# A decoder layer on one core: VectorE reads projection banks ahead of the attention maxima, one weight split moved, unit 1's scores moved into their slab

## The chip, the core and the metric

The kernel runs on one core of a Trainium2 chip. The metric is the device time of one execution in microseconds (us). Before the change it is 679.45 us, the median of three runs (679.43 to 679.52).

## What is computed

One post-norm decoder layer over 512 tokens, model width 1024, float32 in and out. The part of the reference that matters here:

```python
def hybrid_mixer(x, w_in, b_forget, attn_sinks, w_o_fox, w_o_swa, w_out):
    proj = jnp.einsum('bsd,dc->bsc', x, w_in)
    q_f, k_f, v_f, f_logit, q_s, k_s, v_s, g_f, g_s = jnp.split(proj, idx, axis=-1)
    log_f = jax.nn.log_sigmoid((f_logit + b_forget).astype(jnp.float32))
    o_f = forgetting_attention(q_f, k_f, v_f, log_f)        # 8 heads x 64, causal
    qs, ks = apply_rope(q_s, pos), apply_rope(k_s, pos)
    o_s = sliding_window_sink_attention(qs, ks, v_s, attn_sinks)   # 8 q heads, 2 kv heads, window 128
    merged = jax.nn.sigmoid(g_f) * (o_f @ w_o_fox) + jax.nn.sigmoid(g_s) * (o_s @ w_o_swa)
    return jnp.einsum('bsd,de->bse', merged, w_out)

# layer
h = layer_norm(DEEPNORM_ALPHA * h + mix, ln1_g, ln1_b)
ff = (silu(h @ w_gate) * (h @ w_up)) @ w_down
h = layer_norm(DEEPNORM_ALPHA * h + ff, ln2_g, ln2_b)
```

Heads are reshaped from the columns of the projection. The sliding-window softmax takes the maximum of a row and a learned sink, and the sink's exponential joins the denominator.

## The kernel before

Each float32 operand is split in two: a hi part, rounded to the fp32r format that TensorE multiplies (a copy on ScalarE, ACT), and a lo part, the difference (a subtraction on VectorE, DVE). A product is then three matmuls, hi by hi, lo by hi, hi by lo (`mm3`, line 1643).

The weights come as slabs of 128 x 1024 elements. TensorE (PE) works through them in order: slabs 0, 1, 4, 5 give q_s, slabs 2 and 3 k_s, v_s and the forget logits, 6 to 9 q_f, 10 to 13 k_f, 14 to 17 v_f, then gates, output projections and the feed-forward. In slabs 0, 1 and 4 to 13 eight chunks of the model width accumulate in one PSUM bank. ScalarE's `slab_hi` (line 643) and VectorE's `slab_lo` (line 982) prepare slab n+3 in step n; four slabs fit in the ring, and SyncE's queue loads slab n+2 when slab n's lo part is made.

Attention runs beside the projections, in units of one head. There are eight sliding-window units (a = 0 to 7); unit a starts in step 6+a (`unit_step`) and passes through these stages:

- PE in slab 6+a: `scores(a)` (lines 1676, 1681) into banks 2 and 3. For a of 1 and more they wait for the exponentials of unit a-1 (`exp_done`), which read the same banks.
- DVE in step 6+a: `maxima(a)` (line 1153, four custom instructions that add the mask and take the maximum, each with a read of its accumulator). ACT: `exps(a)` (lines 718, 720). DVE: `normalise(a)` (lines 1162 to 1167).
- PE in slab 7+a: `transposes(a)` (line 1706); ACT and DVE take hi and lo parts of the result (`take_probT`, pth at line 741, ptl at line 990).
- PE in slab 8+a: `values(a)` (line 1720); ACT and DVE take the output (`o_low` line 748, `sum_o` line 1183; for an odd unit both heads of the pair are stored by `take_o`). An even unit's sum is written to partitions 0 to 63, an odd unit's to 64 to 127.

On PE a set of slabs, `WITHIN`, places scores and values after two of the slab's eight chunks and transposes after four; in the other slabs scores and values stand ahead of the slab and transposes after two chunks.

The projections' results are read out of their banks in step n by `take(n-1)`: for slabs 6 to 9 ACT copies two halves (line 689), then DVE makes the lo parts (line 1049, `q_f`); for slabs 10 to 13 ACT copies four halves (line 696) and DVE makes the lo parts with line 990 (`kl_f`). Slab n of 8 to 13 uses the bank of slab n-2, so it waits (`qk_taken`) until DVE has read that bank. In steps 6 and 7 DVE also has the rotation of q_s slabs 4 and 5 (`rope_cosine`, `rope_add`, `rope_low`), with ACT's `rope_rotate` (line 659) and `rope_split` (line 666) and a product on GpSimd (POOL, line 585) between.

Every engine works through its instructions in the order written in its own block; the order is all that the loops below decide. There is no scheduler. ACT's loop has, in step n: `take(n-1)`, `take_o_low`, `take_probT`, `exps`, `take_o`, `slab_hi(n+3)`.

Of the kernel before, what the change touches and what calls it, by code (L numbers as in the profile page):

```python
# [49 lines left out]
N_VK = (2, 3)  # L50
N_QF = 6
N_KF = 10
N_V = 14
# [12 lines left out]
AHEAD = SPL - 1  # L66
# [63 lines left out]
def unit_step(a):  # L130

    return 6 + a if a < 8 else 19 + a - 8
# [1 line left out]

WITHIN = tuple(range(unit_step(2), unit_step(7) + 1)) + (unit_step(7) + 2,)


def units_at(n, stage):  # L140

    return [a for a in range(UNITS) if unit_step(a) + stage == n]
# [68 lines left out]
def program(nc, xT, x, slabs, vk_slabs, gu, wdn, rope, rope_tok, sel, b_forget, sinks, ln1_g, ln1_b, ln2_g, ln2_b, out):  # L211
    ctx = ExitStack()
    with ctx:
# [222 lines left out]
        def slot(ring, n, width=D):  # L436
            start = slot_start(n)
            return ring[:, start:start + width]
# [5 lines left out]
        def raw_of(n):  # L444
            if n < FIRST:
                return first_raw[:, n, 0:width_of(n)]
            return raw[:, (n % RAW) * D:(n % RAW + 1) * D]


        def ready(n):  # L450
            return n + 1 if n < N_FF else n + 1 - len(LATE)
# [6 lines left out]
        def width_of(n):  # L458
            return KC // 2 * VK_W if n in N_VK else D
# [518 lines left out]
        def _(dve):  # L978
            def slab_lo(n):
                dve.wait_ge(hi_ready, ready(n))  # L980
                w = width_of(n)
                dve.tensor_tensor(slot(sl, n, w), raw_of(n), slot(sh, n, w).bitcast(F32),  # L982
                                  ALU.subtract).then_inc(lo_ready, 1)
# [5 lines left out]
            def low(dst, src, hi):  # L989
                return dve.tensor_tensor(dst, src, hi.bitcast(F32), ALU.subtract)  # L990
# [47 lines left out]
            def take(n):  # L1038

                b = proj_bank(n)  # L1040
                if n == N_VK[1]:
                    dve.wait_ge(vs_hi, 1)
                    low(v_s[:, :, :, HD:2 * HD], ps[:, VK_BANKS, 0:KV_W].rearrange("p t (g d) -> p t g d", g=2),
                        v_s[:, :, :, 0:HD]).then_inc(vs_taken, 1)
                elif N_QF <= n < N_KF:
                    dve.wait_ge(qk_hi, n - N_QF + 1)
                    for g in range(2):
                        h = 2 * (n - N_QF) + g
                        last = dve.scalar_tensor_tensor(  # L1049
                            out=q_f[half(1 - g), h, :], in0=ps[half(g), b, :], scalar=SCALE,  # L1050
                            in1=q_f[half(g), h, :].bitcast(F32), op0=ALU.mult, op1=ALU.subtract)
                    last.then_inc(qk_taken, 1)
                elif N_KF <= n < N_V:
                    dve.wait_ge(qk_hi, n - N_QF + 1)
                    for g in range(2):
                        last = low(kl_f[half(g), n - N_KF, :], ps[half(g), b, :], kh_f[half(g), 2 * (n - N_KF) + g, :])
                    last.then_inc(qk_taken, 1)
                elif n == N_G - 1:
                    for t in range(TB):
                        dve.wait_ge(v_hi, t + 1)  # L1060
                        low(v_f[:, t, :, HD:2 * HD], ps[:, V_BANKS[t], :].rearrange("p (h d) -> p h d", d=HD),
                            v_f[:, t, :, 0:HD]).then_inc(v_taken, 1)
# [72 lines left out]
            def maxima(a):  # L1135
                b = a % 2
                dve.wait_ge(scores_done, a + 1)
                if a >= 2:
                    dve.wait_ge(exp_done, a - 1)
                j, g = unit_place(a)  # L1140
                if a == 0:
                    dve.wait_ge(consts_made, 8)
                    dve.wait_ge(sink_negated, 1)
                elif a == 8:
                    dve.wait_ge(max_done, 8)
                    dve.memset(masks[:, 2 * P:3 * P], 0.0).then_inc(ahead_zeroed, 1)
                    dve.wait_ge(ahead_zeroed, 1)

                h = j + 4 * g
                least = sink_neg[:, h:h + 1] if a < 8 else -NEG  # L1150
                for i, (bank, col, w, _, _) in enumerate(score_regions(a)):
                    t = ps[:, bank, col:col + w]
                    last = dve.tensor_tensor_reduce(t, t, masks[:, TB * P - w:TB * P], -1.0, least, ALU.add, ALU.min,
                                                    nmax[:, b, i:i + 1])
                last.then_inc(max_done, 1)
# [179 lines left out]
                        rope_add(k)  # L1335

            for n in range(1, N_WOUT + KC - WOUT_TAIL + 1):
                for a in units_at(n, 0):
                    maxima(a)
                if n - 1 in N_QS:  # L1340
                    rope_cosine(n - 1, N_QS.index(n - 1))
                if n == N_QS[-2] + 1:
                    keys_low()
                if n < N_QF:
                    rope_rest(n)
                if n == N_VK[1] + 1:
                    forget_logits()
                    rotate_keys()
                    slab_lo(n - 1 + AHEAD)
                take(n - 1)  # L1350
                for a in units_at(n, 2):
                    sum_o(a)
                if n == N_CUM + 1:
                    take_stacks()
                for a in units_at(n + 1, 0):
                    if a >= 8:
                        head_bias(a - 8)
                for a in units_at(n, 1):
                    take_probT(a)
                if n >= N_QF:  # L1360
                    rope_rest(n)
                if n == N_CUM:
                    bias_stacks()
                for a in units_at(n, 0):
                    normalise(a)
                for a in units_at(n, 2):
                    if a % 2:
                        take_o(a)
                if N_WO < n <= N_WOUT:
                    merge(n - 1 - N_WO)  # L1370
                if n - 1 in N_QS[:2]:
                    rope_add(N_QS.index(n - 1))
                if n != N_VK[1]:
                    slab_lo(n + AHEAD)
                if n >= LATE_STEP:
                    late_slab_lo(n - LATE_STEP)
                if n == N_V:
                    forget_gate()
                if N_WO < n <= N_WOUT:
                    merge_low(n - 1 - N_WO)  # L1380
# [259 lines left out]
        def _(pe):  # L1640
# [133 lines left out]
            def slab(n, between):  # L1774
# [13 lines left out]
                elif N_V <= n < N_G:  # L1788
                    for t in range(TB):
                        if t == 1:  # L1790
                            if n in WITHIN:
                                attend(n)
# [6 lines left out]
                elif n < N_WO:  # L1799
                    for c in range(KC):  # L1800
                        if n in WITHIN:
                            if c == 2:
# [60 lines left out]
            for n in range(2, N_WOUT):  # L1863
                if n not in WITHIN:
                    attend(n)
# [269 lines left out]
```

## Time and profile before

| | us |
|---|---|
| median of three runs | 679.45 |
| the profiled execution, its own time | 679.46 |
| its span in the trace | 677.7 |
| PE busy | 665.8 (98%) |
| DVE busy | 540.3 (80%) |
| ACT busy | 392.2 (58%) |
| POOL busy | 50.8 (7%) |
| mean granted TensorE clock | 0.998 of full speed |

A row of the timeline gives the start and the length of an instruction (or of a merged run of the same instruction), its engine, its line and what it writes and reads; in square brackets stands the idle time of the engine just before it and what ended it. Times count from the start of the span. Matmuls overlap, and their ends are modelled: a row's length is longer than the distance to the next one.

By the chain that ended last PE holds 89% of the span and DVE 5%. It runs through DVE and ACT until 74 us, and from there to 380 us through PE alone.

### The profile page before, as it was taken

Reading aid. Unit: us, or ns where it says so; the run is one execution under the profiler, and the core shown is the slowest. Engines: PE = TensorE matmul, PEld = TensorE weight load, DVE = VectorE, ACT = ScalarE, POOL = GpSimd, SP = SyncE. Lnnn points to the kernel's source line nnn. Section 1 sums busy time; section 2 is a strip of 40 time slices with the busy share of each in tenths; the row PEclk is TensorE's granted clock in tenths of the full one; section 3 lists DMA queues with packets and bytes.
Section 4 is the critical chain, followed back from the end, with each engine's and each line's share of the span. In section 5 each row is a group of like instructions: output and inputs, shape, how many; then the busy total and the mean of one; then the engine's idle time right before and its main releaser. Section 6 shows DMA issues by size and latency. Waiting matters only on the chain.

```text
span 677.7 us, 10965 instructions
## 1 busy us (share of the span) xinstructions
PE 665.8 (98%) x4034; PEld 594.8 (88%) x4034; DVE 540.3 (80%) x1021; ACT 392.2 (58%) x728; POOL 50.8 (7%) x74
## 2 busy tenths in 40 slices
PE   8999999999999999999999999999999999999995
PEld 6977888888888888888899999999999998888884
DVE  5579998767876226655989998888998889998888
ACT  5669687467766244524436555554554558767740
POOL 2102111111001011110200000000000000000000
PEclk9999999999999999999999999999999999999999
DMA  8236667876512886886021244334334327987302
GB/s 314 78 116 171 186 176 213 216 183 164 121 63 95 317 205 168 220 270 200 0 79 60 102 150 155 104 128 155 110 122 155 127 92 249 372 258 208 108 31 93
DMA packets 29560, 107.38 MB, mean 158 GB/s; under 512 B 3616, under 2 KB 3744, under 8 KB 26784
## 3 DMA queue, kind: packets, MB, share of 16 engines
q1 hardware_dynamic: 24624, 79.60, 34.1%
q0 software_dynamic: 4896, 27.28, 16.6%
q8 instruction: 21, 0.34, 0.2%
q14 instruction: 19, 0.16, 0.1%
HBM read 104.77 MB, written 25.17 MB: 192 GB/s over the span
## 4 chain that ended last, share of the span: by engine, by line
PE 89%; DVE 5%; ACT 2%; issue 2%; DMA 1%; POOL 0%; DVEq 0%; SPq 0%; ACTq 0%
PE ps L1643 12%; PE ps L1645 12%; PE ps L1644 12%; PE ps L1960 10%; PE ps L1962 10%; PE ps L1961 10%; PE ps L2028 5%; PE ps L2030 5%; PE ps L2029 5%; PE ps L1720 2%; PE ps L1706 2%; ACT rope L659 1%; PE ps L1681 1%; PE ps L1676 1%; DVE sl L982 1%
## 5 line engine op out<-in xcount | busy, mean ns | idle before, releaser
L982 DVE TENSOR_TENSOR sl<-raw,sh 128x1024 fp32r<-128x1024 f32 x46 | 56.3, 1225 | 43.6 <-ACT sh L643 43.5
L1960 PE MATMUL ps<-hTh,sh 128*128 128x256 f32 x320 | 90.6, 283 | 0.0
L1961 PE MATMUL ps<-hTh,sl 128*128 128x256 f32 x320 | 90.6, 283 | 0.0
L1962 PE MATMUL ps<-hTl,sh 128*128 128x256 f32 x320 | 90.6, 283 | 0.0
L1643 PE MATMUL ps<-xh,sh 128*128 128x512 f32 x208 | 83.6, 402 | 1.1 <-DVE q_f L1049 1.1
L1645 PE MATMUL ps<-xl,sh 128*128 128x512 f32 x208 | 81.3, 391 | 0.0
L1644 PE MATMUL ps<-xh,sl 128*128 128x512 f32 x208 | 81.1, 390 | 0.0
L643 ACT ACTIVATE sh<-raw 128x1024 fp32r<-128x1024 f32 x46 | 48.9, 1064 | 35.6 <-PE ps L1645 22.5
L1960 PE MATMUL ps<-vt,sh 128*128 128x256 f32 x240 | 68.1, 284 | 0.2 <-ACT sg L883 0.2
L1962 PE MATMUL ps<-vt,sh 128*128 128x256 f32 x240 | 67.9, 283 | 0.0
L1961 PE MATMUL ps<-vt,sl 128*128 128x256 f32 x240 | 67.9, 283 | 0.0
L1960 PEld LDWEIGHTS ps<-hTh,sh 128*128 128x128 f32 x320 | 61.4, 192 | 0.0
L1961 PEld LDWEIGHTS ps<-hTh,sl 128*128 128x128 f32 x320 | 61.4, 192 | 0.0
L1962 PEld LDWEIGHTS ps<-hTl,sh 128*128 128x128 f32 x320 | 61.4, 192 | 0.0
L990 DVE TENSOR_TENSOR sl<-raw_f_odd,sh 128x1024 fp32r<-128x1024 f32 (+1 forms) x40 | 43.6, 1090 | 12.8 <-ACT sh L873 12.5
L873 ACT ACTIVATE sh<-raw_f_odd 128x1024 fp32r<-128x1024 f32 (+1 forms) x40 | 38.0, 951 | 19.4 <-DVE raw_f_odd L1440 15.9
L873 ACT ACTIVATE sh<-raw_f_even 128x1024 fp32r<-128x1024 f32 (+1 forms) x40 | 37.9, 950 | 17.0 <-DVE raw_f_even L1440 14.0
L1643 PEld LDWEIGHTS ps<-xh,sh 128*128 128x128 f32 x208 | 39.1, 188 | 9.1 <-issue 2.3
L1645 PEld LDWEIGHTS ps<-xl,sh 128*128 128x128 f32 x208 | 39.0, 188 | 8.6
L1960 PEld LDWEIGHTS ps<-vt,sh 128*128 128x128 f32 x240 | 46.1, 192 | 0.4 <-ACT sg L883 0.4
L990 DVE TENSOR_TENSOR sl<-raw_f_even,sh 128x1024 fp32r<-128x1024 f32 (+1 forms) x40 | 43.4, 1087 | 3.7 <-ACT sh L873 3.4
L1962 PEld LDWEIGHTS ps<-vt,sh 128*128 128x128 f32 x240 | 46.1, 192 | 0.0
(255 smaller groups left out, 1747.6 us busy)
## 6 DMA issues: line engine op xcount, KB each, us to landing
raw<-in_slabs SPq DMA_DIRECT2D x46, 512.0 KB, 4.3
raw_f_even<-in_gu SPq DMA_DIRECT2D x10, 1280.0 KB, 5.4
raw_f_odd<-in_gu SPq DMA_DIRECT2D x10, 1280.0 KB, 5.4
item_raw<-tw SPq DMA_DIRECT2D x44, 256.0 KB, 3.1
item_raw<-in_wdn SPq DMA_DIRECT2D x33, 256.0 KB, 5.6
tw<-in_wdn POOLq DMA_DIRECT2D x11, 512.0 KB, 5.6
tw<-tw POOLq DMA_DIRECT2D x22, 256.0 KB, 4.4
x_raw<-in_xT SPq DMA_DIRECT2D x8, 256.0 KB, 5.8
```

The costliest lines, as they stand in the source:

```text
L643: act.activation(slot(sh, n, width_of(n)), raw_of(n), ACT.Copy).then_inc(hi_ready, 1)
L873: act.activation(sh[:, 512 * at_slot:512 * (at_slot + blocks)], raw_f[k % 2][:, first:first + blocks, :].rearrange("p b n -> p (b n)"), AC ...
L982: dve.tensor_tensor(slot(sl, n, w), raw_of(n), slot(sh, n, w).bitcast(F32), ALU.subtract).then_inc(lo_ready, 1)
L990: return dve.tensor_tensor(dst, src, hi.bitcast(F32), ALU.subtract)
L1643: pe.matmul(dst, lh, rh, start=start, stop=False)
L1644: pe.matmul(dst, ll, rh, start=False, stop=False)
L1645: return pe.matmul(dst, lh, rl, start=False, stop=stop)
L1960: pe.matmul(dst, sh[:, w], bh[:, c, :], start=start and c == 0, stop=False, skip_group_check=True)
L1961: pe.matmul(dst, sl[:, w], bh[:, c, :], start=False, stop=False, skip_group_check=True)
L1962: last = pe.matmul(dst, sh[:, w], bl[:, c, :], start=False, stop=c == KC // 2 - 1, skip_group_check=True)
L2028: pe.matmul(dst, lh, rh, start=start, stop=False, skip_group_check=True)
L2029: pe.matmul(dst, ll, rh, start=False, stop=False, skip_group_check=True)
```

## The change

Three edits. In VectorE's loop, `take(n-1)` stands ahead of `maxima(a)` in steps 7 to 14, where it stood behind. `slab_lo(8)`, which was the last instruction of step 5, stands behind `maxima(0)` in step 6. In the set `WITHIN` slab 7 is added: unit 1's scores move from ahead of slab 7 to behind its second chunk, and unit 0's transposes from behind the second chunk to behind the fourth.

```diff
--- before.py
+++ after.py
@@ -134,7 +134,7 @@
 
 
 
-WITHIN = tuple(range(unit_step(2), unit_step(7) + 1)) + (unit_step(7) + 2,)
+WITHIN = tuple(range(unit_step(1), unit_step(7) + 1)) + (unit_step(7) + 2,)
 
 
 def units_at(n, stage):
@@ -1335,8 +1335,13 @@
                         rope_add(k)
 
             for n in range(1, N_WOUT + KC - WOUT_TAIL + 1):
+
+                if N_QF < n <= N_V:
+                    take(n - 1)
                 for a in units_at(n, 0):
                     maxima(a)
+                if n == N_QF:
+                    slab_lo(n - 1 + AHEAD)
                 if n - 1 in N_QS:
                     rope_cosine(n - 1, N_QS.index(n - 1))
                 if n == N_QS[-2] + 1:
@@ -1347,7 +1352,8 @@
                     forget_logits()
                     rotate_keys()
                     slab_lo(n - 1 + AHEAD)
-                take(n - 1)
+                if not N_QF < n <= N_V:
+                    take(n - 1)
                 for a in units_at(n, 2):
                     sum_o(a)
                 if n == N_CUM + 1:
@@ -1370,7 +1376,8 @@
                     merge(n - 1 - N_WO)
                 if n - 1 in N_QS[:2]:
                     rope_add(N_QS.index(n - 1))
-                if n != N_VK[1]:
+
+                if n not in (N_VK[1], N_QF - 1):
                     slab_lo(n + AHEAD)
                 if n >= LATE_STEP:
                     late_slab_lo(n - LATE_STEP)
```

On DVE, around the start of step 6 (`sl` is a slab's lo part, `kl_s` the keys' lo part, line 1153 the maxima of unit 0), the order changes like this:

```order
 L999 SCALAR_TENSOR_TENSOR rope_even<-ps,cs 128x512
 L990 TENSOR_TENSOR kl_s<-ps,kh_s 64x512 x2
-L982 TENSOR_TENSOR sl<-raw,sh 128x1024
 L1153 ISA ps,nmax<-ps,masks,sink_neg 128x128
 L1153 ISA nmax 128x1
```

The lo part of slab 8 has left the place ahead of the maxima; it stands behind their last accumulator read and ahead of the rotation's `rope_odd`.

On DVE, step 11 before (end of step 10, maxima of unit 5, read of slab 10's bank, o_sum of unit 3), and behind it the same stretch now:

```order
L982 TENSOR_TENSOR sl<-raw,sh 128x1024
L1153 ISA ps,nmax<-ps,masks,sink_neg 128x128
L1153 ISA nmax 128x1
L1153 ISA ps,nmax<-ps,masks,sink_neg 128x256
L1153 ISA nmax 128x1
L1153 ISA ps,nmax<-ps,masks,sink_neg 128x256
L1153 ISA nmax 128x1
L1153 ISA ps,nmax<-ps,masks,sink_neg 128x256
L1153 ISA nmax 128x1
L990 TENSOR_TENSOR kl_f<-ps,kh_f 64x512 x2
L1183 TENSOR_TENSOR o_sum<-ps,o_low 64x512
L990 TENSOR_TENSOR ptl<-ps,pth 128x512
```

```order
L982 TENSOR_TENSOR sl<-raw,sh 128x1024
L990 TENSOR_TENSOR kl_f<-ps,kh_f 64x512 x2
L1153 ISA ps,nmax<-ps,masks,sink_neg 128x128
L1153 ISA nmax 128x1
L1153 ISA ps,nmax<-ps,masks,sink_neg 128x256
L1153 ISA nmax 128x1
L1153 ISA ps,nmax<-ps,masks,sink_neg 128x256
L1153 ISA nmax 128x1
L1153 ISA ps,nmax<-ps,masks,sink_neg 128x256
L1153 ISA nmax 128x1
L1183 TENSOR_TENSOR o_sum<-ps,o_low 64x512
L990 TENSOR_TENSOR ptl<-ps,pth 128x512
```

`kl_f`, which needs ACT's copy of slab 10, stands now between the slab's lo part and the maxima. Steps 7 to 10 have `q_f` (line 1049) in the same two places.

On PE, around the start of slab 7 (scores of unit 1 at lines 1676 and 1681, matmuls of a chunk at 1643 to 1645), before and behind it the same stretch now, where the lines are seven higher:

```order
L1676 MATMUL ps<-kh_s,q_s 128x128
L1676 MATMUL ps<-kh_s,q_s 128x256 x3
L1681 MATMUL ps<-kl_s,q_s 128x128
L1681 MATMUL ps<-kl_s,q_s 128x256 x3
L1643 MATMUL ps<-xh,sh 128x512
L1644 MATMUL ps<-xh,sl 128x512
L1645 MATMUL ps<-xl,sh 128x512
L1643 MATMUL ps<-xh,sh 128x512
L1644 MATMUL ps<-xh,sl 128x512
L1645 MATMUL ps<-xl,sh 128x512
L1706 MATMUL ps<-ident,prob 128x128 x7
```

```order
L1650 MATMUL ps<-xh,sh 128x512
L1651 MATMUL ps<-xh,sl 128x512
L1652 MATMUL ps<-xl,sh 128x512
L1650 MATMUL ps<-xh,sh 128x512
L1651 MATMUL ps<-xh,sl 128x512
L1652 MATMUL ps<-xl,sh 128x512
L1683 MATMUL ps<-kh_s,q_s 128x128
L1683 MATMUL ps<-kh_s,q_s 128x256 x3
L1688 MATMUL ps<-kl_s,q_s 128x128
L1688 MATMUL ps<-kl_s,q_s 128x256 x3
```

Both stretches begin right behind slab 6's last matmul. Slab 7's first two chunks (six matmuls) stand ahead of the scores now, and the transposes of unit 0, which followed those two chunks, come behind the fourth.

## Rows read from the trace of the kernel before

**Rows 1.** Windows; columns: us, busy (x instructions) by engine, clock, DMA share, GB/s
```profile
42.00:74.00 32.00, 30.31 (x161) 24.55 (x159) 27.04 (x73) 24.14 (x62) 6.14 (x7) 1.00 0.53 151
...
108.00:350.00 242.00, 242.00 (x1215) 205.60 (x1214) 159.93 (x319) 126.91 (x228) 28.79 (x37) 1.00 0.58 164
```

**Rows 2.** PE's waits over the span: us in total, times, longest
```profile
PE ps L1643 <- DVE q_f L1049: 1.1, 3, 0.4
...
PE ps L1676 <- ACT prob L720: 0.6, 1, 0.6
```

**Rows 3.** PE timeline, unit 0's scores: start, length, engine, line
```profile
41.78 0.63 PE L1681 MATMUL ps<-kl_s,q_s 128*128 128x128 f32 x4
```

**Rows 4.** DVE timeline, steps 6 and 7
```profile
43.26 1.34 DVE L982 TENSOR_TENSOR sl<-raw,sh 128x1024 fp32r<-128x1024 f32 x1 [2.12 <-ACT sh L643]
44.63 0.36 DVE L1153 CUSTOM_DVE_ANT_0 ps<-ps,masks,sink_neg 128x128 f32<-128x128 f32 x1
...
53.22 0.35 DVE L1153 CUSTOM_DVE_ANT_0 ps<-ps,masks,sink_neg 128x128 f32<-128x128 f32 x1
...
54.87 1.39 DVE L1049 SCALAR_TENSOR_TENSOR q_f<-ps,q_f 64x512 fp32r<-64x512 f32 x2
56.30 1.15 DVE L990 TENSOR_TENSOR ptl<-ps,pth 128x512 fp32r<-128x512 f32 x2
```

**Rows 5.** ACT timeline, steps 7, 10, 11 and 12
```profile
53.12 1.20 ACT L689 ACTIVATE q_f<-ps 64x512 fp32r<-64x512 f32 x2
...
80.59 0.30 ACT L718 ACTIVATE esink<-nmax,sink_sb 128x4 f32<-128x4 f32 x1
...
82.38 0.23 ACT L720 ACTIVATION_READ_ACCUMULATOR prob<-ps,nmax 128x1 f32 x1
82.47 1.08 ACT L643 ACTIVATE sh<-raw 128x1024 fp32r<-128x1024 f32 x1
83.42 2.41 ACT L696 ACTIVATE kh_f<-ps 64x512 fp32r<-64x512 f32 x4
...
90.59 0.66 ACT L754 ACTIVATE o_s<-o_sum 128x512 fp32r<-128x512 f32 x1
91.11 1.09 ACT L643 ACTIVATE sh<-raw 128x1024 fp32r<-128x1024 f32 x1
```

**Rows 6.** DVE timeline, steps 8 to 11
```profile
62.03 0.35 DVE L1153 CUSTOM_DVE_ANT_0 ps<-ps,masks,sink_neg 128x128 f32<-128x128 f32 x1
...
65.11 0.68 DVE L1183 TENSOR_TENSOR o_sum<-ps,o_low 64x512 f32<-64x512 f32 x1
...
70.84 0.35 DVE L1153 CUSTOM_DVE_ANT_0 ps<-ps,masks,sink_neg 128x128 f32<-128x128 f32 x1
...
75.71 0.15 DVE L1162 TENSOR_TENSOR den<-den,esink 128x4 f32<-128x4 f32 x1
...
78.84 0.35 DVE L1153 CUSTOM_DVE_ANT_0 ps<-ps,masks,sink_neg 128x128 f32<-128x128 f32 x1
...
86.10 0.35 DVE L1153 CUSTOM_DVE_ANT_0 ps<-ps,masks,sink_neg 128x128 f32<-128x128 f32 x1
...
87.58 0.14 DVE L1153 DVE_READ_ACCUMULATOR2_ANT nmax<- 128x1 f32 x1
87.58 1.39 DVE L990 TENSOR_TENSOR kl_f<-ps,kh_f 64x512 fp32r<-64x512 f32 x2
89.01 0.69 DVE L1183 TENSOR_TENSOR o_sum<-ps,o_low 64x512 f32<-64x512 f32 x1
89.72 1.16 DVE L990 TENSOR_TENSOR ptl<-ps,pth 128x512 fp32r<-128x512 f32 x2
```

**Rows 7.** PE timeline: scores of units 5 and 7, values of unit 6
```profile
83.62 0.63 PE L1676 MATMUL ps<-kh_s,q_s 128*128 128x128 f32 x4
...
99.86 0.63 PE L1676 MATMUL ps<-kh_s,q_s 128*128 128x128 f32 x4
...
106.62 0.28 PE L1720 MATMUL ps<-pth,v_s 128*128 128x256 f32 x1
```

## Prediction

> Steps are passes of the VectorE and ScalarE loops; step n also stands for slab n on TensorE. Unit a (0 to 7) has its scores in step 6+a. DVE, ACT and PE are the engines' names in the rows.
>
> **What bounds the kernel now.** First the windows: PE is busy 30.31 of 32 us between 42 and 74, and all 242 of 242 us between 108 and 350 [rows 1]. So what the eight units of steps 6 to 13 cost PE is the only thing the change can touch, and a delay of PE there reaches the end: nothing later waits for anything else. Then PE's waits over the span: 1.1 us in three waits of a slab's first matmul for DVE's q_f, and 0.6 us in one wait of scores for ACT's exponentials [rows 2]. The three are the starts of slabs 8, 9 and 10; the fourth is that of unit 1's scores. They are 1.7 us by the rows, and a little more in truth, since matmuls overlap and their ends are modelled; I count 1.7 as what could be won. Then DVE's timeline: it waits ahead of the lo parts of slabs 8 and 9 and nowhere in steps 7 to 9. A DVE step is 8.81 us there (53.22 to 62.03, and 62.03 to 70.84), a PE step without waits 8.12 us ((99.86 - 83.62) / 2) [rows 4, 6, 7]. The order on DVE thus decides, and there the change acts.
>
> **Part 1: slab 8's lo part behind unit 0's maxima.** DVE waits 2.12 us until 43.26 for slab 8's hi part, and the maxima start at 44.63 [rows 4]. The scores are done at 41.78 + 0.63 = 42.41 [rows 3]. Maxima start at 42.45: 2.18 us earlier. The exponentials, ACT's rotation, slab 9's hi and lo parts follow in one chain and move by the same 2.18 us. Slab 8's lo part now ends some 0.6 us later, near 45.2; PE needs it at about 55, so it costs nothing. DVE gets 2.18 us of lead. Bounds: 0 (something unseen held the scores) to 2.18 us; I take 2.18, since PE's row is the nearest thing to a measurement of it.
>
> **Part 2: unit 1's scores inside slab 7.** The exponentials of unit 0 now end near 46.2 (maxima from 42.45, 1.65 us, then 2.02 us for the exponentials), over 1.5 us before slab 6 does on PE. So part 1 has already removed the wait, and scores two chunks later gain nothing more; alone, part 2 would have covered it too. No DVE or ACT work waits for it (maxima of unit 1 start after 53).
>
> **Part 3: take(n-1) ahead of maxima(a) in steps 7 to 14.** The slab's bank is free about 1.6 us earlier (the 1.65 us of maxima are no longer ahead of its reader), which removes the three stalls. But the maxima now stand behind DVE's q_f or kl_f, which waits for ACT's copy of the slab, and the next unit's scores wait for the exponentials of this one. I follow this chain with durations of rows and 0.03 to 0.05 us for each handing over.
>
> Step 7. ACT's q_f copy of slab 6 starts at 53.12 - 2.18 = 50.94 and ends at 52.14 [rows 5]. DVE's q_f starts at 52.17, takes 1.42, maxima(1) start at 53.59 (before: 53.22) and end 1.62 later (87.58 + 0.14 - 86.10) [rows 6], exponentials from 55.25, 2.02 long (82.38 + 0.23 - 80.59) [rows 5], done 57.27. Scores of unit 2 start at 57.32. PE, which has shed waits of 0.6 and 0.4 us with their restarts, comes to them near 56.3: a new wait of about 1 us stands in for the old ones.
>
> Step 8. Behind the maxima (1.49) the rest of step 7 on DVE is 62.03 - 56.30 = 5.73 [rows 4, 6]: 60.81. ACT's copy hangs on the same DVE step (its rope_split waits for rope_add) and is done some 0.1 us later; q_f 60.94, maxima(2) 62.36, exponentials 64.03.
> Step 9. 62.36 + 1.49 + (70.84 - 65.11 = 5.73) = 69.58 [rows 6]: q_f, maxima(3) 71.00, exponentials 72.66, done 74.68.
> Step 10. Normalisation waits for these: 74.72 + (78.84 - 75.71 = 3.13) = 77.85 [rows 6]; maxima(4) 79.27, exponentials 80.93, which is 0.34 us behind before's 80.59 [rows 5]. Scores of unit 5 at 80.93 + 2.02 + 0.05 = 83.00 against 83.62 [rows 7]: a gain of 0.6 us is all that is left.
>
> Steps 11 to 13, where k is read. ACT's copy has four parts. From one unit's exponentials to the next's there is now a closed loop: exponentials 82.47 - 80.59 = 1.88, slab's hi part 83.42 - 82.47 = 0.95, k copy 2.41, handing over 0.03, kl_f 89.01 - 87.58 = 1.43, maxima 1.62, handing over 0.03: 8.35 us; behind an odd unit's sum_o also 91.11 - 90.59 = 0.52: 8.87 us [rows 5, 6]. PE's step is 8.12, so PE waits in each. Exponentials(5) start at 80.93 + 8.35 = 89.28, (6) at + 8.87 = 98.15, and scores(7) at 98.15 + 2.07 = 100.22 against 99.86: PE is now 0.4 us behind before. Exponentials(7) start at + 8.35 = 106.50.
> Step 14. values(6) stand ahead of slab 14 and need DVE's last ptl of unit 6. It stands behind maxima(7), which start 1.65 earlier, at 104.85. Then o_sum at 106.50 (1.65, see below), ptl at + 0.71 = 107.21, 1.16 long [rows 6]: 108.37. values(6) start at 108.5 against 106.62 [rows 7]: 1.85 us late. With some 0.08 us for a restart from idle it is 1.9 us, and part 3 has cost 4 us of the 2.2 that part 1 gave.
>
> Maxima to o_sum isn't in the trace. The nearest rows are 1.65 (53.22 to 54.87, before q_f) and 1.48 (86.10 to 87.58, before kl_f) [rows 4, 6]. I take 1.65: like q_f's first half, this o_sum of an odd unit writes the upper partitions; the gap to ptl behind one is 89.72 - 89.01 = 0.71. With 1.48 the sum is 0.17 less. q_f to maxima isn't there either; q_f to ptl is 1.43, kl_f to o_sum 1.43: 1.42 taken; if the maxima could overlap as they do behind a lo part, 0.09 less in each of seven steps, 0.6 us.
>
> The Trainium skill ("VectorE: DVE Perf Modes", section "Two Vector instructions with no wait between them") says that a Vector instruction whose operand starts in another quadrant of partitions than the last one in that memory starts only when all earlier ones have finished. By that rule both handings over are held: 1.65 and 1.42, which is the sum above; without it 0.8 us less. The trace agrees as far as the two distances 1.65 and 1.48 go.
>
> POOL's rotation product and its chain of tw transfers start up to 2.18 us earlier. Cost 0: nobody on PE waits for them before 350 [rows 1]; and all slab copies of these steps come long after their loads. PE's clock is 1.00 in both windows [rows 1], and I take it for the new waits of 1 to 1.5 us too.
>
> **Sum.** The profiled execution took 679.46 us (span 677.7 and 1.76 around it), the median of the runs is 679.45. 679.46 + 1.9 = 681.4 us.
>
> **Rivals.**
> A. The forecast; own range 680.8 to 682.2 (0.6 below by the two handings over, 0.8 above for small handings over in 20 places of the chain).
> B. Faster: no loop closes. If ACT's copies of q and k were there as soon as DVE comes to them, maxima start in time in steps 7 to 13 and the 1.7 us of stalls vanish with nothing in their place: 677.8. It decides in step 8: exponentials(1) must end before 56.3, where PE comes to the scores of unit 2. For it: in steps 7 to 10 the closed loop is only 1.88 + 0.95 + 1.20 + 0.03 + 1.43 + 1.62 + 0.03 = 7.14 us, under PE's 8.12. Against: DVE's own steps of 8.81 us, and ACT's copy in step 7 ends at 52.14 whatever DVE does.
> C. The three q_f stalls turn into waits for exponentials as above, but the k steps cost nothing, because DVE had been ahead: the 0.6 us stay, 678.9. Against: ACT's 2.41 us, behind its exponentials in the same queue.
> D. The k loop bites, but DVE's tail in step 14 doesn't: only the 0.4 us of scores(7) and a part of the rest: 680.2.
> E. Part 1 gives nothing, since the maxima start no earlier (scores done later than PE's modelled end says): part 3's cost alone, 679.46 + 1.9 + 2.18 = 683.5.
>
> **Numbers.** A 0.76, B 0.04, C 0.06, D 0.07, E 0.07. A measurement here can tell a change beyond 0.2%, 1.36 us: slower is above 680.82, faster below 678.10. Of A some 0.07 lies below 680.82. Slower 0.69 + 0.07 = 0.76 (E); faster 0.04 and a bit of C, 0.05; same 0.19. The range leaves out B, C and E (0.17): 680.0 to 682.6.
>
> **What would show it.** Right: maxima(0) near 42.5, no PE wait for q_f any more, but scores of units 2, 3, 4, 5, 6, 7 waiting for ACT's prob, the longest at units 2 and 7; DVE waiting for kh_f by about 0.7 us in steps 11 to 13; values(6) waiting over a microsecond for ptl near 107; PE without waits from there to 350. Wrong: scores of unit 7 before 99.9, or kl_f never waiting; or q_f waits still in PE's list.

## The result: 0.44% slower, and the profile after

The changed kernel takes 682.17 us (median of 6 runs, 681.51 to 683.53), the kernel before 679.44 us in the runs beside it (6 runs, 678.89 to 680.29). The ratio is 1.0044, interval 1.0031 to 1.0057. The forecast was 681.4 us, slower; its own range was 680.8 to 682.2, the one with the rivals' shares 680.0 to 682.6. The measured time lies 0.03 us inside the first. The profiled execution took 681.85 us with a span of 680.1 us, 2.4 us more than before.

PE's waits over the span after; columns: us in total, times, longest. The scores stand at line 1683 now, the values at 1727.

```profile
PE ps L1683 <- ACT prob L720: 2.3, 4, 1.0
PE ps L1727 <- DVE ptl L990: 1.3, 1, 1.3
```

The three waits for q_f of [rows 2] are gone, as part 3 meant, and so is the one of unit 1's scores. In their place stand four waits for exponentials and one for ptl: 3.6 us for 1.7 us.

The windows after, to set beside [rows 1]; columns as there:

```profile
42.00:74.00 32.00, 30.65 (x165) 25.65 (x163) 28.09 (x75) 23.83 (x60) 6.23 (x8) 1.00 0.56 166
74.00:108.00 34.00, 32.53 (x184) 26.97 (x182) 30.23 (x83) 26.46 (x69) 5.75 (x8) 1.00 0.68 177
108.00:350.00 242.00, 241.09 (x1204) 204.66 (x1205) 160.34 (x323) 126.94 (x233) 28.62 (x37) 1.00 0.58 164
```

PE's clock is 1.00 in all three; behind 108 us only the last 0.9 us of the wait for ptl is missing from PE's busy time.

PE's timeline after, from unit 0's scores to unit 7's transposes: the rows of the places where it stopped, and a neighbour where the stop shows only in the distance. Columns as in [rows 3], with the idle time in brackets.

```profile
40.98 0.70 PE L1683 MATMUL ps<-kh_s,q_s 128*128 128x128 f32 x4
...
57.18 0.73 PE L1683 MATMUL ps<-kh_s,q_s 128*128 128x128 f32 x4 [0.98 <-ACT prob L720]
...
82.70 0.39 PE L1652 MATMUL ps<-xl,sh 128*128 128x512 f32 x1
83.09 0.73 PE L1683 MATMUL ps<-kh_s,q_s 128*128 128x128 f32 x4
...
100.58 0.73 PE L1683 MATMUL ps<-kh_s,q_s 128*128 128x128 f32 x4 [0.62 <-ACT prob L720]
...
108.91 0.38 PE L1727 MATMUL ps<-pth,v_s 128*128 128x256 f32 x1 [1.30 <-DVE ptl L990]
...
111.35 0.38 PE L1713 MATMUL ps<-ident,prob 128*128 128x128 f32 x2
```

The waits in the list are units 2, 3, 4 and 7. Units 5 and 6 waited too, but so shortly that the list has no entry: scores(5) start 0.39 us behind the last matmul where others follow at 0.23, and their first group is 0.73 long, as in the rows with a wait, where it is 0.63 without one [rows 7]. Scores(6) start 0.47 us behind the matmul ahead.

I use one distance from here on: from the start of scores(0) to the start of transposes(7). PE does the same work between the two in every version. It is 111.35 - 40.98 = 70.37 us after, and 108.95 - 41.24 = 67.71 us before: +2.66 us. The two rows of before, on PE's timeline:

```profile
41.24 0.70 PE L1676 MATMUL ps<-kh_s,q_s 128*128 128x128 f32 x4
...
108.95 0.82 PE L1706 MATMUL ps<-ident,prob 128*128 128x128 f32 x6
```

What lies ahead of scores(0) is not the change's: that start falls anywhere from 40.98 to 43.05 us in the profiled executions of this case. Behind transposes(7) all of them take the same time to the end of the span, 568.66 to 568.94 us, so a difference in the distance reaches the end.

### The profile page after: what moved, and what is told of

Read it like the earlier page. It is cut to its first block, busy times and chain, and to the rows that moved or that the text cites. A ratio compares the mean times of both kernels' runs of the same rounds, so it can differ in the third digit from the quotient of the medians.

```text
span 680.1 us, 10965 instructions
## 1 busy us (share of the span) xinstructions
PE 666.8 (98%) x4034; PEld 594.9 (87%) x4034; DVE 541.3 (80%) x1021; ACT 392.5 (58%) x728; POOL 50.7 (7%) x74
## 4 chain that ended last, share of the span: by engine, by line
PE 87%; DVE 6%; ACT 4%; issue 2%; DMA 1%; DVEq 0%; SPq 0%; ACTq 0%
PE ps L1650 12%; PE ps L1652 12%; PE ps L1651 12%; PE ps L1967 10%; PE ps L1969 10%; PE ps L1968 10%; PE ps L2035 5%; PE ps L2036 5%; PE ps L2037 5%; PE ps L1727 2%; PE ps L1713 1%; DVE ps L1153 1%; ACT prob L720 1%; PE ps L1683 1%; ACT kh_f L696 1%
## 5 line engine op out<-in xcount | busy, mean ns | idle before, releaser
L1968 PEld LDWEIGHTS ps<-vt,sl 128*128 128x128 f32 x240 | 46.1, 192 | 0.0
```

What stands on the lines that cost most here:

```text
L1968: pe.matmul(dst, sl[:, w], bh[:, c, :], start=False, stop=False, skip_group_check=True)
```

## The experiments

"Distance" is scores(0) to transposes(7) in each version's own trace, with the difference to before. The ratios are to runs of the kernel before taken beside each version's own.

| version | median us (runs) | ratio, interval | distance us |
|---|---|---|---|
| before | 679.44 (6) | | 67.71 |
| the change, all parts | 682.17 (6) | 1.0044, 1.0031 to 1.0057 | 70.37, +2.66 |
| e1 part 3 alone | 684.81 (5) | 1.0074, 1.0061 to 1.0087 | 72.41, +4.70 |
| e2 parts 1 and 2 | 677.05 (5) | 0.9964, 0.9951 to 0.9977 | 65.66, -2.05 |
| e6 part 1 alone | 677.34 (6) | 0.9963, 0.9949 to 0.9977 | 65.65, -2.06 |
| e10 part 2 alone | 679.37 (11) | 0.9997, 0.9986 to 1.0009 | 67.69, -0.02 |
| e3 all, part 3 in steps 7 to 10 only | 679.86 (11) | 1.0009, 1.0000 to 1.0017 | 67.52, -0.19 |
| e4 all, part 3 in steps 11 to 14 only | 679.74 (12) | 1.0004, 0.9996 to 1.0013 | 67.86, +0.15 |
| e5 all, slab n+3 out of the loop | 680.54 (12) | 1.0012, 1.0002 to 1.0023 | 68.63, +0.92 |
| e7 all, values(6) inside slab 14 | 681.77 (10) | 1.0031, 1.0020 to 1.0041 | 70.42, +2.71 |
| e9 the changed kernel once more | 683.29 (6) | 1.0047, 1.0033 to 1.0061 | 70.35, +2.64 |
| e11 all, unit 7's maxima first | 682.24 (9) | 1.0031, 1.0020 to 1.0042 | 69.34, +1.63 |
| e12 all, unit 1's maxima first | 681.68 (8) | 1.0030, 1.0019 to 1.0042 | 69.35, +1.64 |
| e8 parts 1 and 2, rope_low later | 677.18 (6) | 0.9959, 0.9943 to 0.9975 | 65.00, -2.71 |

Medians of different sets of runs differ by some tenths to over 1 us for the same order of instructions (e9 and the change: 683.29 and 682.17), while the distances of these two agree to 0.02 us. So the ratios say whether a version is faster or slower than before, and the distances say by how much and where; the ratios' intervals are some 0.1% to either side, and can't order the change, e7, e11 and e12 among each other.

### The change in its parts: e1, e2, e6, e10

e1 has only the lines with `take`, e2 only the other two edits. Expected of e1:

> Only the bank reads ahead of the maxima (steps 7 to 14); slab 8's lo part and slab 7's scores as before. Chain theory (maxima behind the bank reads, loop closed over ScalarE): the lead of 2.18 us that the moved lo part gives is missing, so the cost shows in full: about +4.8 us, 684.3 us against 679.5. Rival 1 (the loss sits in step 14 alone, where values of unit 6 wait for ptl, 1.3 us): about +1.3 to +2. Rival 2 (the three stalls at slab starts are really won): about 0 or faster.

Of e2:

> Slab 8's lo part behind unit 0's maxima and slab 7 in WITHIN, bank reads behind the maxima as before. Chain theory: VectorE's whole chain of steps 6 to 9 starts 2.2 us earlier and nothing gives it back: -2.2 us, about 677.3, with one stall of 0.4 us left at slab 10. Rival (the lead runs into another wait): -0.8 to 0.

PE's waits in e1, then in e2, of the places that the parts touch:

```profile
PE ps L1681 <- ACT prob L720: 3.2, 3, 2.0
PE ps L1725 <- DVE ptl L990: 1.3, 1, 1.3
```

```profile
PE ps L1647 <- DVE q_f L1049: 0.4, 1, 0.4
```

The parts add up: +4.70 and -2.05 give 2.65, and the whole change measures 2.66. Part 3 alone costs 4.7 us (4.8 expected); parts 1 and 2 give 2.05 us (2.2 expected). One of the four waits of before is left in e2's list, at the start of slab 10.

There is one more thing in e1. Behind the wait of scores(2), PE's granted clock fell to the lower of its two levels (0.50 of full speed) from 61.8 to 65.2 us. The row of the wait, and a window behind it with the columns of [rows 1]:

```profile
60.14 0.73 PE L1681 MATMUL ps<-kh_s,q_s 128*128 128x128 f32 x4 [1.98 <-ACT prob L720]
```

```profile
62.00:65.00 3.00, 3.00 (x10) 2.31 (x10) 2.96 (x6) 2.28 (x4) 0.81 (x1) 0.50 0.21 41
```

From scores(2) to scores(3) it is 9.83 us there (60.14 to 69.97), against 8.12 for a step without a stop at a clock of 1.00: 1.7 us of PE's time. It doesn't reach the distance. PE would have waited for VectorE and ScalarE in these steps anyway, and from scores(2) to scores(7) it is 43.38 us in e1 (60.14 to 103.52) and 43.40 in the changed kernel (57.18 to 100.58). So the 4.70 us are what the order costs.

e6 keeps unit 1's scores where they were, e10 moves nothing but them:

```diff
 e6:
-WITHIN = tuple(range(unit_step(1), unit_step(7) + 1)) + (unit_step(7) + 2,)
+WITHIN = tuple(range(unit_step(2), unit_step(7) + 1)) + (unit_step(7) + 2,)
 both, in VectorE's loop:
-                if N_QF < n <= N_V:
-                    take(n - 1)
...
-                if not N_QF < n <= N_V:
-                    take(n - 1)
+                take(n - 1)
 e10 also:
-                if n == N_QF:
-                    slab_lo(n - 1 + AHEAD)
...
-                if n not in (N_VK[1], N_QF - 1):
+                if n != N_VK[1]:
```

> Part 1 alone: slab 8's lo part behind unit 0's maxima; unit 1's scores stay where they were, take stays behind the maxima. Theory: the lead of 2.2 us is all that parts 1 and 2 together gave (677.05 measured with both), part 2 is worth nothing: 677.1 us, and no wait of scores for prob at unit 1. Rival, part 2 carries a share (the wait of unit 1's scores was 0.6 us before): 677.7, with a wait of some 0.5 us at scores(1).

> Part 2 alone: unit 1's scores two chunks inside slab 7; slab 8's lo part and take as before. Theory: the 0.6 us wait of scores(1) for prob goes, but VectorE's step is as late as it was, so the q_f wait at the start of slab 8 grows from 0.35 to about 0.9 us with what TensorE won: 679.4 us, no change. Rival, the wait that goes is a gain of its own: 678.8.

e6 equals e2 in its distance (65.65 and 65.66): part 2 adds nothing to part 1. Alone it is worth nothing either, -0.02 us. PE's timeline of e10 around the start of slab 8, and its waits for q_f:

```profile
58.07 0.47 PE L1643 MATMUL ps<-xh,sh 128*128 128x512 f32 x1 [1.29 <-DVE q_f L1049]
```

```profile
PE ps L1643 <- DVE q_f L1049: 2.1, 3, 1.3
```

The 0.6 us wait of unit 1's scores is gone [rows 2], and the first wait for q_f has grown from 0.35 to 1.29 us. I had expected 0.9. The distance is the same, so what PE gained was handed back in full; that the list then shows 2.1 us in three waits for the same loss as 1.7 us in four fits with a wait that costs more than its entry (see below, e8). The rival is out.

### Which steps cost: e3 and e4

Both have parts 1 and 2; the read stands ahead of the maxima only where q_f is read (e3) or only where kl_f is read (e4).

```diff
 e3:
-                if N_QF < n <= N_V:
+                if N_QF < n <= N_KF:
 e4:
-                if N_QF < n <= N_V:
+                if N_KF < n <= N_V:
```

> All of the change, but bank reads ahead of the maxima in steps 7 to 10 only (q_f). Chain theory: four waits for exponentials (1.0, 0.4, 0.4, 0.1 us), no loop over the k copies: -0.2 us, about 679.3, the same as before; scores of units 6 and 7 and values of unit 6 don't wait. Rival (the loss comes from the first steps already): +1 or more.

> All of the change, but bank reads ahead of the maxima in steps 11 to 14 only (kl_f). Chain theory: the lead of 2.2 us reaches step 11 and covers most of the k loop: +0.2 us, 679.7, with waits at scores of unit 7 (0.5) and values of unit 6 (1.4). Rival (k loop costs a fixed sum whatever the lead): as e3 loses 2 to 2.7 us less than the full change, this one would be at -2.2 + 2.9 = +0.7.

PE's waits in e3, then in e4:

```profile
PE ps L1683 <- ACT prob L720: 1.7, 3, 1.0
```

```profile
PE ps L1727 <- DVE ptl L990: 1.3, 1, 1.3
...
PE ps L1650 <- DVE q_f L1049: 0.4, 1, 0.4
PE ps L1683 <- ACT prob L720: 0.3, 1, 0.3
```

Both came as expected: -0.19 and +0.15 us for -0.2 and +0.2, in e4 with 0.3 us at unit 7 where 0.5 was expected.

Against e2, the q steps cost 67.52 - 65.66 = 1.86 us, the k steps 67.86 - 65.66 = 2.20 us. Together they cost 4.71, that is 0.65 us more than the two apart. In e3 the list has no wait for prob behind unit 4 (it has units 2, 3 and 4): VectorE makes its lateness good in the k steps as long as the read stands behind the maxima there. In e4 the k steps begin with VectorE in time, and only unit 7 waits, 0.3 us. In the changed kernel they begin late, and pay from the first step on. This refutes rival C (k steps free: e4 would then equal e2) and rival D (tail free: e4 shows the tail's 1.3 us alone).

### The loop, shortened: e5

The forecast says that the steps which read k are bound by a closed loop over ScalarE and VectorE, longer than PE's 8.12 us. Slab n+3's hi part is in that loop (0.95 us on ACT). e5 puts it, and its lo part on VectorE, behind the next step's read and maxima:

```diff
 ScalarE's loop, behind take(n - 1):
+                if N_KF < n <= N_V:
+                    slab_hi(n - 1 + AHEAD)
...
-                slab_hi(n + AHEAD)
+                if not N_KF <= n < N_V:
+                    slab_hi(n + AHEAD)
 VectorE's loop, behind maxima(a):
+                if N_KF < n <= N_V:
+                    slab_lo(n - 1 + AHEAD)
...
-                if n not in (N_VK[1], N_QF - 1):
+                if n not in (N_VK[1], N_QF - 1) and not N_KF <= n < N_V:
```

> All three parts, but in steps 10 to 13 the next slab's hi part (ScalarE) stands behind the bank read of the following step, and its lo part (VectorE) behind the following maxima. The loop theory: the hi part's 0.95 us leaves the path from one unit's exponentials to the next's, which falls from 8.5 and 9.0 us to some 7.5 and 8.1, at or under TensorE's 8.12. The waits of scores 6 and 7 for prob go; what is left is the start (scores 2 to 4) and the tail (values(6) for ptl, about 1.4 us). 680.6 us, some 1.5 less than with all parts as they are, 1.2 above before. Rival, the length of the loop doesn't matter and the delay comes from the maxima's later place in VectorE's own queue: the waits of scores 6 and 7 stay, 682.0.

ACT's timeline after, units 4 to 6, then the same places in e5: the first instruction of the exponentials, and the copies behind them.

```profile
83.87 2.41 ACT L696 ACTIVATE kh_f<-ps 64x512 fp32r<-64x512 f32 x4
...
89.51 0.30 ACT L718 ACTIVATE esink<-nmax,sink_sb 128x4 f32<-128x4 f32 x1 [1.10 <-DVE nmax L1153]
...
91.40 0.64 ACT L754 ACTIVATE o_s<-o_sum 128x512 fp32r<-128x512 f32 x1
91.92 1.06 ACT L643 ACTIVATE sh<-raw 128x1024 fp32r<-128x1024 f32 x1
```

```profile
81.30 0.30 ACT L718 ACTIVATE esink<-nmax,sink_sb 128x4 f32<-128x4 f32 x1 [1.01 <-DVE nmax L1156]
...
83.20 2.40 ACT L696 ACTIVATE kh_f<-ps 64x512 fp32r<-64x512 f32 x4
85.63 1.06 ACT L643 ACTIVATE sh<-raw 128x1024 fp32r<-128x1024 f32 x1
...
88.83 0.30 ACT L718 ACTIVATE esink<-nmax,sink_sb 128x4 f32<-128x4 f32 x1 [0.15 <-DVE nmax L1156]
...
96.90 0.30 ACT L718 ACTIVATE esink<-nmax,sink_sb 128x4 f32<-128x4 f32 x1
```

In the changed kernel the exponentials of units 4 to 7 start at 81.03, 89.51, 98.52 and 106.99: steps of 8.48, 9.01 and 8.47 us. In e5 they start at 81.30, 88.83, 96.90 and 104.81, steps of 7.53, 8.07 and 7.91, where 7.5 and 8.1 were expected; ScalarE waits 0.15 us for the maxima where it waited 1.10. PE's waits in e5:

```profile
PE ps L1688 <- ACT prob L720: 1.8, 3, 1.0
...
PE ps L1732 <- DVE ptl L993: 0.8, 1, 0.8
```

Units 6 and 7 wait no more, the rest is the start (units 2 to 4 in the list) and the tail, 0.8 us where I expected 1.4. The distance is 1.74 us shorter than with all parts (1.5 expected). From scores(4) to scores(7) PE takes 24.74 us in e5 (74.98 to 99.72) against 25.88 after, 1.14 less; the rest of the gain is at the tail. That the loop's length sets the k steps is shown. e5 takes VectorE's lo part away from ahead of kl_f as well; in the changed kernel VectorE stood idle for 0.53 to 0.62 us behind it, waiting for ScalarE's kh_f, so there it was not what held kl_f.

### The tail: e7, e9 and e11

e7 lets values(6) stand two chunks inside slab 14, so that PE would have work while ptl is made:

```diff
-WITHIN = tuple(range(unit_step(1), unit_step(7) + 1)) + (unit_step(7) + 2,)
+WITHIN = tuple(range(unit_step(1), unit_step(7) + 3))
```

> All three parts, and values(6) stand two chunks inside slab 14 in place of ahead of it, so TensorE has 1.7 us of other work while ptl is made. Theory: the 1.3 us wait for ptl in front of slab 14 goes, and a shorter one for the bank or the next exponentials takes a part of it: 681.3 us, 0.85 less than with all parts as they are. Rival, slab 14 itself waits for its bank as long as values(6) did: 682.1. Second rival, the whole wait goes: 680.8.

It is nothing: 70.42 against 70.37. PE's and ACT's timelines of e7 at slab 14:

```profile
107.71 0.39 PE L1652 MATMUL ps<-xl,sh 128*128 128x512 f32 x1
109.59 0.47 PE L1650 MATMUL ps<-sh,xh 128*128 128x512 f32 x1 [1.49 <-issue]
```

```profile
107.48 0.30 ACT L718 ACTIVATE esink<-nmax,sink_sb 128x4 f32<-128x4 f32 x1 [1.10 <-DVE nmax L1153]
...
109.28 0.21 ACT L720 ACTIVATION_READ_ACCUMULATOR prob<-ps,nmax 128x1 f32 x1
```

The trace names no releaser, but the code has one that fits: slab 14 is the first whose bank is one of the scores' banks, and `bank_free(14)` waits for all eight exponentials (`exp_done, 8`). These end at 109.28 + 0.21 = 109.49, 0.10 us before the matmul. So two chains hang on unit 7's maxima, one through ptl to values(6), one through the exponentials to slab 14, and they end within 0.2 us of each other (counted from scores(0): values(6) start at 67.93 us after, slab 14 at 68.08 in e7). Taking the first away uncovers the second. The gain of 0.85 us that I expected isn't there; the first of the two rivals is what came.

e11 and e9 ask how much of the tail is the order in its own step. e9 was to do this by leaving the last step out of the edit; but VectorE's step 14 has no maxima, so its condition changed no instruction's place, and e9 is the changed kernel once more. For the same reason the change itself alters VectorE's order in steps 7 to 13 only. The step it should have named is 13, as e11 does.

```diff
 e9:
-                if N_QF < n <= N_V:
+                if N_QF < n < N_V:
 e11:
-                if N_QF < n <= N_V:
+                if N_QF < n < N_V - 1:
```

> All three parts, but take stays behind the maxima in the last of the eight steps, step 14 (take ahead in steps 7 to 13 only). It parts the tail's wait in what the order of step 14 itself costs and what the lateness handed down by the k steps costs. Theory, both count: VectorE is free at 103.2 us, so maxima(7) start there in place of 105.2, kl_f follows at about 104.9, o_sum 1.43 later, ptl at 107.1 in place of 107.7. values(6) still wait, 0.7 us in place of 1.3, and the median is 681.6. Rival, the order of step 14 is the whole tail: no wait at values(6), 680.8. Second rival, it is nothing: 682.2.

> All three parts, but in VectorE's step 13, which holds the last maxima of the eight units (unit 7's), the maxima stand ahead of the bank read again; the read stays ahead in steps 7 to 12. Theory: VectorE is free for them at 103.2 us in place of waiting for kl_f until 105.2, and unit 6's ptl, two instructions behind, comes 0.7 to 1.0 us sooner, at 106.8 to 107.0. The wait of values(6) shrinks from 1.3 to 0.4 to 0.6 us but does not go, since the steps before are as late as they were: 681.3 us. Rival, the order of this one step is the whole tail: no wait at values(6), 680.8. Second rival, it is nothing: 682.2.

VectorE's timeline of e11 in step 13, and PE's waits there:

```profile
104.00 1.22 DVE L982 TENSOR_TENSOR sl<-raw,sh 128x1024 fp32r<-128x1024 f32 x1
105.14 0.35 DVE L1153 CUSTOM_DVE_ANT_0 ps<-ps,masks,sink_neg 128x128 f32<-128x128 f32 x1
...
106.62 1.38 DVE L990 TENSOR_TENSOR kl_f<-ps,kh_f 64x512 fp32r<-64x512 f32 x2
108.03 0.68 DVE L1183 TENSOR_TENSOR o_sum<-ps,o_low 64x512 f32<-64x512 f32 x1
108.75 1.15 DVE L990 TENSOR_TENSOR ptl<-ps,pth 128x512 fp32r<-128x512 f32 x2
```

```profile
PE ps L1683 <- ACT prob L720: 2.4, 4, 1.0
...
PE ps L1727 <- DVE ptl L990: 0.3, 1, 0.3
```

kl_f no longer waits, the maxima start straight behind the lo part. Counted from scores(0) (43.05 here), ptl starts at 65.70 against 66.72 after (107.70 - 40.98), and the wait is 0.3 in place of 1.3 us. The whole is 1.03 us shorter, at the upper end of what I expected. So of the 1.3 us that the list gives PE's wait at the tail, 1.0 is the order of step 13 and 0.3 is handed down; by the distances from scores(7) to values(6), 8.33 us after, 7.34 in e11 and 6.76 before, it is 1.0 and 0.6 (a wait costs more than its entry, see e8).

### The start: e12

The same for the first of the steps, 7 (`N_QF + 1 < n <= N_V`):

> All three parts, but in step 7, which holds unit 1's maxima, they stand ahead of q_f again; the read stays ahead in steps 8 to 13. Theory: exponentials(1) end in time and the 1.0 us wait of scores(2) goes, but the loop from step to step is as it was, so the waits of scores 3 and 4 stay and grow by what TensorE won, and all that is behind comes some 0.9 us sooner: 681.2 us. Rival, the delay is made anew in the loop of the k steps whatever the q steps hand down: scores(7) and the tail where they were, 682.0.

```profile
PE ps L1683 <- ACT prob L720: 1.6, 3, 0.7
...
PE ps L1727 <- DVE ptl L990: 1.3, 1, 1.3
```

Unit 2's wait of 0.98 us goes, unit 3's grows from 0.37 to 0.66, units 4 and 7 and the tail wait as before. The distance is 1.02 us shorter (0.9 expected). In this kernel, where the later loops leave no slack, the delay of step 7 is a plain addend.

### A version that beats both: e8

e2 still has the 0.4 us wait at slab 10. e8 is e2 with one piece of the rotation on VectorE (`rope_low` of slab 5) moved from step 8 to step 10.

```diff
-                    if n == m + 2 + (k >= 2):
+                    if n == (m + 2, m + 2, m + 3, m + 5)[k]:
```

> Parts 1 and 2 without part 3, and one rope_low piece of VectorE moved from step 8 to step 10, where it has slack. Theory: the last q_f wait (slab 10, 0.4 us) goes and nothing comes in its place: 676.6 us, the least of all versions, 2.8 below before. Rival, the moved piece delays the exponentials of a later step and a wait for prob comes up: 677.0 or above.

Its window, to set beside the first of [rows 1]:

```profile
42.00:74.00 32.00, 32.00 (x178) 27.41 (x177) 28.40 (x80) 26.79 (x67) 6.38 (x8) 1.00 0.57 170
```

PE is busy 32.00 of 32 us, and the list has no wait left for q_f, prob or ptl, though the median alone (677.18) would have spoken for the rival. By the distance it is 2.71 us faster than before and 0.66 faster than e2. The medians of e2, e6 and e8 (677.05, 677.34, 677.18) can't order the three; all are faster than before, by 0.4%.

The theory that nothing stays is almost true. A stop too short for the list is left at the start of slab 9, and e2, e4 and e6 have it too. PE's timeline of e8:

```profile
63.32 0.39 PE L1649 MATMUL ps<-xl,sh 128*128 128x512 f32 x1
63.66 0.47 PE L1647 MATMUL ps<-xh,sh 128*128 128x512 f32 x1
```

They start 0.34 us apart, where others follow at 0.23, and VectorE's q_f, for which slab 9 waits, ends at 63.51 (62.12 + 1.39). From scores(2) to scores(3) it is 8.33 us, in the next steps 8.12: the stop costs 0.21 us.

PE's steps also say what a wait costs. Without a wait a step is 8.12 us. Before, the steps with q_f waits of 0.41 and 0.39 us are 8.81 us each (scores at 57.88, 66.69 and 75.50); after, the step with a prob wait of 0.37 us is 8.76 (65.94 to 74.70). So a wait costs 0.27 to 0.30 us more than its entry. Of this 0.16 is the modelled end of the matmul ahead (0.39 long, the next one 0.23 behind it), from which the idle time is counted, and about 0.1 the longer first group or matmuls. The four waits of before, 1.7 us in the list [rows 2], thus come to 2.9 us; e8 wins 2.71 of them and keeps the 0.21 at slab 9. The same count holds after: 3.6 us in five listed waits and 0.27 more for each make 5.0, and the two that the list leaves out cost 0.27 us (unit 5, a step of 8.39) and about 0.34 (unit 6: 0.47 less 0.23, and 0.1 for the group), 5.6 in all; the distance is 70.37 - 65.00 + 0.21 = 5.58 above e8's without its stop.

## Why the prediction was right, and where it was short

- **Part 1** was to give 2.18 us. The maxima of unit 0 start at 42.20 (42.45 forecast, and the run's scores(0) were 0.26 earlier), behind a wait for the scores themselves. Counted from scores(0) they start 2.17 us earlier (1.22 for 3.39). With this lead two of the four waits go, the one at slab 9 shrinks to the short stop, the one at slab 10 stays, and e6 gains 2.06 us. The prediction counted 1.7 us as all that could be won; by e8 it is at least 2.71, and rival B's time would have had to be 676.7 or less. That term was read off the list, which gives a wait for less than it costs.
- **Part 2**, worth 0: 0.02 us alone, 0.01 on top of part 1.
- **Part 3** was to cost some 4 us; it costs 4.71. Its mechanism is the one forecast, step for step: no wait for q_f, waits of scores for exponentials, the longest at units 2 and 7, VectorE waiting 0.53 to 0.62 us for kh_f (0.7 forecast), a wait of 1.3 us for ptl. The distance grew by 2.66 us where the forecast had 1.9; these 0.76 us have two addends. PE's clock, taken as 1.00 behind the new waits, stayed there; only the longer wait of e1 brought it down. The times of the changed kernel that are compared with forecast ones in the next item have 0.26 us added, for the earlier start of that run.
- First addend, **+0.36 us up to unit 4's exponentials** (81.29 for 80.93). At q_f it is 0.12 in step 7 (52.29 for 52.17), 0.11 in step 8 (61.05 for 60.94), 0.23 in step 9 (69.81 for 69.58) and 0.34 in step 10 (78.19 for 77.85). The first 0.12 stand already in ScalarE's copy, for which VectorE waits there, and come from unit 0: from the first maximum to the exponentials it is 43.97 - 42.20 = 1.77 us, where it was 46.29 - 44.63 = 1.66 before (the second addend has the same term). The next two increments are one mis-sized term, the lo part ahead of q_f: from a slab's lo part to the maxima it was 78.84 - 77.70 = 1.14 in step 10 before, and to q_f it is 1.25:

VectorE's timeline after, step 10:

```profile
76.68 1.22 DVE L982 TENSOR_TENSOR sl<-raw,sh 128x1024 fp32r<-128x1024 f32 x1
77.93 1.39 DVE L1049 SCALAR_TENSOR_TENSOR q_f<-ps,q_f 64x512 fp32r<-64x512 f32 x2
```

- Second addend, **+0.39 us in the loop of the k steps**: 8.48, 9.01 and 8.47 for 8.35, 8.87 and 8.35. The term is "maxima 1.62, handing over 0.03": behind kl_f the exponentials start 1.78 us after the maxima.

VectorE's timeline after, step 11; to set beside the maxima of [rows 6]:

```profile
86.31 1.39 DVE L990 TENSOR_TENSOR kl_f<-ps,kh_f 64x512 fp32r<-64x512 f32 x2 [0.62 <-ACT kh_f L696]
87.73 0.36 DVE L1153 CUSTOM_DVE_ANT_0 ps<-ps,masks,sink_neg 128x128 f32<-128x128 f32 x1
88.11 0.08 DVE L1153 DVE_READ_ACCUMULATOR2_ANT nmax<- 128x1 f32 x1
88.11 0.49 DVE L1153 CUSTOM_DVE_ANT_0 ps<-ps,masks,sink_neg 128x256 f32<-128x256 f32 x1
...
89.33 0.14 DVE L1153 DVE_READ_ACCUMULATOR2_ANT nmax<- 128x1 f32 x1
89.50 0.68 DVE L1183 TENSOR_TENSOR o_sum<-ps,o_low 64x512 f32<-64x512 f32 x1
```

From the first to the second custom instruction it is 88.11 - 87.73 = 0.38 us here. In e11, where the maxima of step 13 stand behind the lo part again, kl_f follows the start of the maxima by 1.48 us (105.14 to 106.62), and o_sum here by 1.77. kl_f to maxima is 87.73 - 86.31 = 1.42, exactly the value taken; for maxima to o_sum I took 1.65. So the rule cited (a Vector instruction whose operand starts in another quadrant than the last one in that memory waits for all earlier ones; the Trainium skill, "VectorE: DVE Perf Modes", section "Two Vector instructions with no wait between them") was right to be counted in both places. The sums of even units show the other side: where o_sum writes the lower partitions, it follows the start of the maxima by 1.59 us (96.75 to 98.34, step 12) in place of 1.77. What the sum left out is the hold in two further places, the two distances that I had too short, 0.11 us each. q_f's first half writes the other half of the partitions (`q_f[half(1 - g)]` in `take`) than the lo part ahead of it, kl_f's first half the same one, and in e4 kl_f follows the lo part by 1.13 us (83.71 to 84.84) where q_f takes 1.25. The first accumulator read starts its write in the lower partitions; behind kl_f and kl_s, whose second halves write the upper ones, it and the second maximum come 0.10 to 0.11 us later than behind q_f, whose second half writes the lower ones. The rows fit the rule in every case that I compared, but no run moves an operand to another quadrant and changes nothing else, so that it is the cause is argued from these rows.
- What I called step 14 at the tail is PE's slab 14; unit 7's maxima, o_sum and that ptl are in VectorE's step 13. The times don't depend on the name, but e9 does: it took the name for VectorE's.
- Of the rivals, B falls with the waits that came up, C and D with e4, E with e6.

## What to carry to other kernels

Reordering a queue to remove another engine's wait can cost more than the wait, since the queue now waits for something else (here 4.7 us for waits of 1.7 in the list). Look for the closed loop: if what is moved ahead needs a third engine, and this engine's work needs what was moved behind, the step becomes the sum of both, to be compared with the bound engine's step (here 8.5 to 9.0 us against 8.12). Giving an engine a lead (2 us from moving one split) was worth more than any other reordering tried here (e5 gave 1.74 on top of the change), and the two must be measured apart: here the change that won was shipped inside one that lost.

## What the runs showed of the hardware

- How soon the maxima's first accumulator read and the second maximum follow goes with the partitions that VectorE wrote just before. Over all traces the second maximum starts 0.37 to 0.39 us after the first behind kl_f or kl_s (34 rows), whose second half is written to the upper partitions, and 0.26 to 0.28 us behind a slab's lo part (all partitions, from the lowest) or q_f, whose second half is written to the lower ones (78 rows). A lo part followed by q_f, which starts by writing the upper partitions, takes 1.24 to 1.26 us (24 rows), by kl_f 1.13 (e4, the one row without a wait).
- A group of PE's first matmuls after a wait is some 0.1 us longer (0.73 for 0.63), with the clock at 1.00, and a wait's entry in the list is 0.16 us too small. The waits that the list gives as 0.37 to 0.41 us lengthened PE's step by 0.64 to 0.69.
- PE's granted clock fell to 0.50 in e1 behind a wait of 1.98 us in a busy stretch, and stood there from about 61.8 to 65.2 us. Behind the waits of 1.29 (e10), 1.30 (after) and 1.49 us (e7) it stayed at 1.00.
- In five profiled executions (e2, e9, e10, e11, e12) PE's mean granted clock is 0.96 in the first 42 us, ahead of anything that the edits touch; it stands at 0.50 for some 3 to 4 us between 7 and 13 us. Just before, PE had waited 1.4 to 1.9 us in all for ScalarE's first hi parts, against 0 to 1.2 us in the others, where the clock is 1.00. In the five scores(0) start at 42.26 to 43.05 us, in the others at 40.98 to 42.02. It is one reason why executions of one program differ by a microsecond: of e9's six runs the four with a mean clock of 0.994 took 683.05 to 683.78 us, the two with 0.998 took 681.70 and 681.98.
